# A square-relu MLP whose relu and token factor become one VectorE operation from the accumulators, and two RMS norms at a layer border joined

## The chip, the cores and the metric

The kernel runs on one core of a Trainium2 chip. The metric is the device time of one execution in microseconds, as the median of several runs. PE is TensorE (matmul), PEld its weight load, DVE is VectorE, ACT ScalarE, POOL GpSimd, and SP the engine that issues most of the transfers.

## The reference, cut to what matters

Two model parts run one after the other on 512 tokens of width 1024, in fp32. The first has two layers, each a mixer (attention, then a gated linear attention, GLA) and an MLP; it ends with a norm. The second begins with a norm of its own.

```
def rmsnorm(x, g):
    y = x * rsqrt(mean(x * x, axis=-1) + EPS)
    return y * g

def sq_relu_mlp(h, w_in, w_out):              # 1024 -> 4096 -> 1024
    return square(relu(h @ w_in)) @ w_out

# first part, for each of two layers
h = h + mixer(rmsnorm(h, norm_mix[i]))
h = h + sq_relu_mlp(rmsnorm(h, norm_mlp[i]), mlp_w_in[i], mlp_w_out[i])
# end of the first part, begin of the second
x = rmsnorm(h, final_norm)
hn = rmsnorm(x, norm_g[0]) * (1.0 + sc1) + sh1
y = hybrid_mixer(hn, ...)
x = x + g1 * rmsnorm(y, norm_g[1])
```

`sc1`, `sh1` and `g1` come from a conditioning vector; a matrix product for it, called ada here, is computed on POOL beside the MLPs.

## The kernel before, in words

The program is written out by hand for each engine, with semaphores between them; nothing reorders it. Activations lie transposed: features on the 128 partitions, 8 tiles of 512 tokens. Every fp32 product is made of three faster fp32r matmuls from high and low parts (`three`, L252 to L254): data and weights are split by ACT, which rounds the high part (`split_hi`, L214, for weights), and by DVE, which subtracts (`split_lo`, L222). A weight block is 128x2048 and has two slots. Its users count `block_done`.

**The MLP** has 16 units of 256 hidden features. PE does, in turn, `in(u)` (48 matmuls of 512 columns into two PSUM banks) and `out(u-1)` (four quarters, each of 12 matmuls into two banks, banks 4-5 and 6-7 in turn). A quarter is added to the residual `x` by DVE (`mlp_dve_add`, L808), and quarters 2 and 3 can start only once the add of the quarter two before has freed its banks. The token factor 1/rms of the norm is not in the input of `in`: it is multiplied in afterwards, from `rstd`. For a unit, ACT takes relu from the accumulators into `m_r` (L775), DVE multiplies by `rstd` (L816), DVE squares in place (L818), ACT rounds to `m_hi` (L778), and DVE subtracts to `m_lo` (L825). In its queue DVE has, for each unit: L816, L818, the add of quarter 0, `split_lo` for the next block, the add of quarter 1, L825, the adds of quarters 2 and 3, `split_lo`.

**A norm's sum** is numbered by `n`. ACT squares pairs of tiles (L320); for the numbers in `FOLDED` POOL adds the pairs (L343), and PE then makes 4 matmuls with a matrix of ones (L333) where it would make 8 otherwise. Each is an fp32 matmul, of which the trace shows two instructions. ACT makes `rstd` by Ln and Exp (L348, L349).

**The border** between the parts lies behind the second MLP: sum 4 of the last quarters, `rstd`, then `dve_norm_x` (L387), which writes the normed `x` tile by tile; PE sums up ada (L1200); ACT squares the new `x`, PE makes sum 5 (not folded), ACT makes `rstd` again; then per tile DVE makes a row (L370), ACT rounds it into `h_hi` (L361) and DVE subtracts into `h_lo` (L380), and PE starts on the mixer's first block. The mixer (`mix_*`) has first four blocks with rotary products (`rotate`, L1275), scores of an index head (`index_score`, L1298), whose relu ACT takes (L1480) and DVE adds up, a top-k on DVE, and then 48 attention steps, in which DVE takes the maximum of a step's scores (L1699), ACT its exponential (L1505), and PE fills the time with projection blocks.

Of the kernel before, what the change touches and what calls it, by code (L numbers as in the profile page):

```python
# [23 lines left out]
P = 128  # L24
# [55 lines left out]
def build(nc, xT_d, wb_d, ada_d, prm_d, con_d, rope_d, gup_d, rel_d, sel_d, out_d):  # L80
    with ExitStack() as ctx:
# [70 lines left out]
        with ExitStack() as scope:  # L152
# [14 lines left out]
            with ExitStack() as s2:  # L167
                with ExitStack() as s3:
                    mx.update({n: sb(n, s, F32, s3) for n, s in [("x_qi", [P, 2, S]), ("x_ki", [P, 1, S])]})
                mx.update({n: sb(n, s, d, s2) for n, s, d in [  # L170
                    ("b_q2", [P, 4, S], F32R), ("b_k2", [P, 4, S], F32R), ("b_kl", [P, 4, S], F32R), ("b_v", [P, TT, 4, P], F32),
                    ("c_v", [P, TT, 2, P], F32), ("x_o", [P, 2, S], F32)]})
# [123 lines left out]
        def squares(n):  # L296


            return ff["f_c"] if n == 7 else sq

        FOLDED = (1, 2, 3, 4, 6, 8)
# [81 lines left out]
        def dve_norm_x(dve, n, gain):  # L383

            dve_rstd(dve, n)
            for k in range(KT):
                dve.scalar_tensor_tensor(out=x[:, k, :], in0=x[:, k, :], scalar=gain[:, k:k + 1], in1=rstd[:],  # L387
                                         op0=ALU.mult, op1=ALU.mult).then_inc(n_app, 1)
# [102 lines left out]
        def attn_pe(pe):  # L491
# [224 lines left out]
        m_relu, m_scaled, m_sq, m_hi, m_lo, m_out, m_add = map(sem, ("m_relu", "m_scaled", "m_sq", "m_hi_s", "m_lo_s", "m_out", "m_add"))  # L716
# [52 lines left out]
        def mlp_act_in(act, i, u, par, b, slot, more=True):  # L769
# [107 lines left out]
        def gla_pe(pe, b0, rows):  # L877
# [10 lines left out]
            def within(h):  # L888

                for d in range(2):  # L890
# [338 lines left out]
        X_UNITS = 48  # L1229
        F_LOG, CUM = mx["x_o"][0:4, 0, :], mx["x_o"][0:4, 1, :]  # L1230
# [38 lines left out]
        def mix_pe(pe, b0):  # L1269
# [31 lines left out]
            pe_block(pe, b0, b0 % 2, HH, 0, rows=40)  # L1301
# [7 lines left out]
            rotate(1)  # L1309
            pe.wait_ge(x_raw, 2)  # L1310
# [3 lines left out]
            pe.wait_ge(x_tok, 1)  # L1314
            for k in range(2, KT):
# [116 lines left out]
        def mix_act(act, b0):  # L1432
# [40 lines left out]
            next_hi(act, b0 + 4, b0 % 2)  # L1473

# [99 lines left out]
        def mix_dve(dve, b0):  # L1574
# [132 lines left out]
            for s in range(X_UNITS + 3):  # L1707
# [352 lines left out]
def program(nc, block, e):  # L2060
# [68 lines left out]
    def _(act):  # L2129
# [17 lines left out]
        e["act_std"](act, 3, 6)  # L2147
        e["mlp_act"](act, 1, B_MLP1, 4)
# [15 lines left out]
    def _(dve):  # L2164
# [12 lines left out]
        e["ada_dve"](dve, 0)  # L2177
        e["gla_dve"](dve, B_GLA)
# [16 lines left out]
    def _(pe):  # L2195
# [10 lines left out]
        e["pe_sums"](pe, 5, 2)  # L2206
# [145 lines left out]
```

## Time and profile before

| | us |
|---|---|
| median of 3 runs | 2146.72 (2146.18 to 2148.09) |
| the profiled execution's own time | 2146.94 |
| its span in the trace | 2145.2 |
| PE busy | 2064.4 (96%) |
| DVE busy | 1161.0 (54%) |
| ACT busy | 748.6 (35%) |
| POOL busy | 583.8 (27%) |

The 1.7 us between the span and the time of the same execution lie around the program. A busy share is an average over stages. Idle time of PE is what can be won; work taken from another engine counts only where PE waits for it.

### The profile page before, as it was taken

The numbers are of one execution on the slowest core, as the hardware profiler recorded it, in microseconds if no ns is written. First come the engines' busy times: TensorE is split into PE (matmuls) and PEld (weight loads), VectorE is DVE, ScalarE is ACT, GpSimd is POOL, SyncE is SP. The second block draws the span as 40 slices with busy tenths as digits, with TensorE's granted clock in tenths as the row PEclk, the third lists the DMA queues.
The fourth block names the chain that finished last, engine by engine and source line by source line (L and its number), as shares of the span: only waits on it lengthen the run. The fifth ranks groups of instructions, "written<-read, shape, count | busy, mean of one in ns | idle before, by whom it ended". The sixth has DMA issues, their size and how long they took to land.

```text
span 2145.2 us, 23937 instructions
## 1 busy us (share of the span) xinstructions
PE 2064.4 (96%) x9444; PEld 1641.4 (77%) x9444; DVE 1161.0 (54%) x1163; ACT 748.6 (35%) x783; POOL 583.8 (27%) x478
## 2 busy tenths in 40 slices
PE   8999999999999998999999998999999979999996
PEld 5666777777777887777777776788888858888884
DVE  4687455655655445455655654594235354545455
ACT  4455432222225432332222223345553233322322
POOL 0000189994000000189994001233320000000000
PEclk9999999999999999999999998999999989999998
DMA  4200144442222231134442222132222312222221
GB/s 173 87 20 1 40 150 145 148 148 95 98 79 81 79 98 40 40 141 153 149 146 96 98 79 84 60 79 64 75 79 98 107 51 99 80 96 98 98 98 39
DMA packets 30812, 197.81 MB, mean 92 GB/s; under 512 B 3312, under 2 KB 3440, under 8 KB 7952
## 3 DMA queue, kind: packets, MB, share of 16 engines
q1 hardware_dynamic: 25552, 168.44, 23.0%
q0 software_dynamic: 5184, 28.31, 4.0%
q8 instruction: 53, 0.87, 0.2%
q14 instruction: 23, 0.19, 0.0%
HBM read 191.50 MB, written 2.10 MB: 90 GB/s over the span
## 4 chain that ended last, share of the span: by engine, by line
PE 85%; DVE 7%; issue 4%; ACT 3%; POOL 1%; DMA 0%; DVEq 0%; POOLq 0%; ACTq 0%; SPq 0%
PE ps L252 23%; PE ps L254 22%; PE ps L253 22%; PE ps L551 3%; PE ps L333 2%; DVE x L808 2%; PE ps L538 1%; PE ps L1391 1%; PE ps L283 1%; PE ps L285 1%; PE ps L284 1%; PE ps L941 1%; PE ps L530 1%; PE ps L529 1%; DVE m_r L816 1%
## 5 line engine op out<-in xcount | busy, mean ns | idle before, releaser
L222 DVE TENSOR_TENSOR w_lo<-w_raw,w_hi 128x2048 fp32r<-128x2048 f32 x140 | 326.4, 2332 | 218.1 <-ACT w_hi L214 216.5
L214 ACT ACTIVATE w_hi<-w_raw 128x2048 fp32r<-128x2048 f32 x144 | 275.3, 1912 | 411.7 <-PE ps L254 411.6
L252 PE MATMUL ps<-h_hi,w_hi 128*128 128x512 f32 x944 | 382.2, 405 | 11.8 <-DVE h_lo L380 7.8
L253 PE MATMUL ps<-h_lo,w_hi 128*128 128x512 f32 x944 | 373.6, 396 | 0.0
L254 PE MATMUL ps<-h_hi,w_lo 128*128 128x512 f32 x944 | 372.9, 395 | 0.0
L343 POOL TENSOR_TENSOR sq<-sq 128x1024 f32<-128x1024 f32 x12 | 38.6, 3218 | 857.6 <-ACT sq L320 857.6
L1184 POOL TENSOR_SCALAR ada_t<-ada_w,prm 128x256 f32<-128x256 f32 x192 | 259.1, 1349 | 10.4 <-DMA ada_w<-in_ada 9.5
L252 PEld LDWEIGHTS ps<-h_hi,w_hi 128*128 128x128 f32 x944 | 181.2, 192 | 56.7 <-issue 20.2
L252 PE MATMUL ps<-m_hi,w_hi 128*128 128x512 f32 x512 | 205.4, 401 | 6.5 <-DVE x L808 6.4
L254 PEld LDWEIGHTS ps<-h_hi,w_lo 128*128 128x128 f32 x944 | 180.7, 191 | 39.2
L253 PEld LDWEIGHTS ps<-h_lo,w_hi 128*128 128x128 f32 x944 | 181.3, 192 | 37.5 <-issue 1.4
L252 PE MATMUL ps<-m_xhi,w_hi 128*128 128x512 f32 x512 | 203.6, 398 | 0.0
L254 PE MATMUL ps<-m_xhi,w_lo 128*128 128x512 f32 x512 | 203.3, 397 | 0.0
L254 PE MATMUL ps<-m_hi,w_lo 128*128 128x512 f32 x512 | 203.0, 397 | 0.0
L253 PE MATMUL ps<-m_lo,w_hi 128*128 128x512 f32 x512 | 201.6, 394 | 0.0
L253 PE MATMUL ps<-m_xlo,w_hi 128*128 128x512 f32 x512 | 201.5, 393 | 0.0
L816 DVE TENSOR_TENSOR m_r<-m_r,rstd 128x1024 f32<-128x1024 f32 x32 | 43.2, 1349 | 248.7 <-ACT m_r L775 248.7
L808 DVE TENSOR_TENSOR x<-x,ps 128x1024 f32<-128x1024 f32 x128 | 155.3, 1214 | 30.1 <-PE ps L254 30.1
L1191 POOL TENSOR_TENSOR ada_acc<-ada_acc,ada_t 128x256 f32<-128x256 f32 x168 | 160.5, 956 | 14.0
L775 ACT ACTIVATE m_r<-ps 128x1024 f32<-128x1024 f32 x32 | 32.9, 1027 | 273.4 <-PE ps L254 273.3
L252 PEld LDWEIGHTS ps<-m_hi,w_hi 128*128 128x128 f32 x512 | 96.1, 188 | 41.3 <-DVE x L808 19.9
L253 PEld LDWEIGHTS ps<-m_xlo,w_hi 128*128 128x128 f32 x512 | 96.1, 188 | 25.1 <-issue 1.0
(278 smaller groups left out, 3335.9 us busy)
## 6 DMA issues: line engine op xcount, KB each, us to landing
w_raw<-in_wb SPq DMA_DIRECT2D x154, 1024.0 KB, 4.9
ada_w<-in_ada POOLq DMA_DIRECT2D x24, 1024.0 KB, 5.4
x<-in_xT SPq DMA_DIRECT2D x4, 512.0 KB, 5.1
out_T<-x SPq DMA_DIRECT2D x4, 512.0 KB, 2.8
b_k<-b_k POOLq DMA_DIRECT2D x4, 256.0 KB, 5.5
b_kl<-b_kl POOLq DMA_DIRECT2D x4, 256.0 KB, 6.7
con<-in_con SPq DMA_DIRECT2D x1, 640.0 KB, 11.4
a_kh<-a_kh POOLq DMA_DIRECT2D x2, 256.0 KB, 3.7
```

Of the source, the lines that this page charges most:

```text
L214: act.activation(w_hi[:, slot], w_raw[:, slot], ACT.Copy).then_inc(hi_done, 1)
L222: dve.tensor_tensor(w_lo[:, slot], w_raw[:, slot], w_hi[:, slot].bitcast(F32), ALU.subtract).then_inc(split_done, 1)
L252: pe.matmul(out, w[0], h[0], start=start, stop=False)
L253: pe.matmul(out, w[0], h[1], start=False, stop=False)
L254: return pe.matmul(out, w[1], h[0], start=False, stop=stop)
L333: last = pe.matmul(ps[:, bank, :], ones[:], squares(n)[:, slot, i * S:(i + 1) * S], start=(j == (2 if folded else 0) and i == 0), stop=(j ...
L343: pool.tensor_tensor(sq[:, 0], sq[:, 0], sq[:, 1], ALU.add).then_inc(n_fold, 1)
L551: pe.matmul(ps[:, h % 2, :], at_["a_v"][:, c, kv, :], p_turned[:, half, :][:, c, :], start=c == 0, stop=c == TT - 1).then_inc(a_PV, 1)
L808: dve.tensor_tensor(xd, xd, pair_(2 + q % 2), ALU.add).then_inc(m_add, 1)
L816: dve.tensor_tensor(two(r), two(r), rstd[:].unsqueeze(1).to_broadcast([P, 2, S]), ALU.mult).then_inc(m_scaled, 1)
L1184: pool.tensor_scalar(ml["ada_t"][:, k % 2], w, cact[:, k:k + 1], None, ALU.mult).then_inc(ada_row, 1)
L1191: ins = pool.tensor_tensor(acc, acc, ml["ada_t"][:, k % 2], ALU.add)
```

## The change

It has three parts. **In the MLP**, one `scalar_tensor_tensor` on DVE reads the accumulators and makes max(0, v) times `rstd`; the squares move to ACT, twice: one rounded into `m_hi`, one in place in `m_r`. ACT's relu and copy go, and ACT's weight split stands ahead of both. **At the border**, sum 4 is taken over x squared times the squared gain of `final_norm` plus a small number, so that its `rstd` serves both norms at once; the rows of `h` are made straight from the old `x` with the product of both gains (`G_BOTH`). Sum 5, of plain squares, now folded, gives the factor `x_r4` of the first norm, which only `x` itself needs: its squares stand behind the rows on ACT, its matmuls behind the second rotary product on PE, and `dve_norm_x` is spread over attention steps 32 to 39. **Small things**: the gains and constants lie in columns of the identity matrix `con`, so that transposes use `identr`, a copy; two short helpers make the gains, on DVE ahead of GLA and on ACT ahead of the second MLP.

```diff
+        FOLDED = (1, 2, 3, 4, 5, 6, 8)
...
+            if n == 4:
+                for i in range(2):
+                    ins = act.activation(to[:, i, :], src[:, 2 * j + i, :], ACT.Square, scale=G_ROOT[:, 2 * j + i:2 * j + i + 1])
+            else:
+                ins = act.activation(to, src[:, 2 * j:2 * j + 2, :], ACT.Square)
+            ins.then_inc(n_sq, 1)
...
         def act_std(act, n, bank):
 
             act.wait_ge(n_ssq, ssq_before(n + 1))
-            alink(act, act.activation(rstd[:], ps[:, bank, :], ACT.Ln, bias=pc("eps"), scale=1.0 / D))
-            act.activation(rstd[:], rstd[:], ACT.Exp, scale=-0.5).then_inc(n_std, 1)
+            to = X_R4[:] if n == 5 else rstd[:]
+            alink(act, act.activation(to, ps[:, bank, :], ACT.Ln, bias=EPS2 if n == 4 else pc("eps"), scale=1.0 / D))
+            act.activation(to, to, ACT.Exp, scale=-0.5).then_inc(n_std, 1)
...
+        def dve_norm_x(dve, n, gain, k):
+
+            if k == 0:
+                dve_rstd(dve, n)
+            dve.scalar_tensor_tensor(out=x[:, k, :], in0=x[:, k, :], scalar=gain[:, k:k + 1], in1=X_R4[:],
+                                     op0=ALU.mult, op1=ALU.mult).then_inc(n_app, 1)
+
+        def both_gains_dve(dve):
+
+            gf = pc("final", 0, KT)
+            dve.memset(EPS2, EPS * EPS)
+            dve.tensor_tensor(G_ROOT, gf, gf, ALU.mult)
+            dve.tensor_tensor(G_BOTH, gf, gain2[:, 0, :], ALU.mult).then_inc(g_both, 1)
+            dve.wait_ge(g_both, 1)
+
+        def both_gains_act(act):
+
+            act.wait_ge(g_both, 1)
+            alink(act, act.activation(G_ROOT, G_ROOT, ACT.Ln, bias=pc("eps")))
+            alink(act, act.activation(G_ROOT, G_ROOT, ACT.Exp, scale=0.5))
...
             act.wait_ge(block_done, b + 1)
-            if not (isinstance(u, int) and i == 0 and u < 2):
-                act.wait_ge(m_lo, c - 1)
-            act.activation(ml["m_r"][:, par].rearrange("p (a s) -> p a s", a=2), pair_(par), ACT.Relu).then_inc(m_relu, 1)
             split_hi(act, b + 2, slot)
-            act.wait_ge(m_sq, c + 1)
-            act.activation(ml["m_hi"][:, par], ml["m_r"][:, par].rearrange("p (a s) -> p a s", a=2), ACT.Copy).then_inc(m_hi, 1)
+            act.wait_ge(m_relu, c + 1)
+            r = two(ml["m_r"][:, par])
+            act.activation(ml["m_hi"][:, par], r, ACT.Square)
+            act.activation(r, r, ACT.Square).then_inc(m_hi, 1)
...
-            dve.wait_ge(m_relu, c + 1)
+            dve.wait_ge(block_done, b + 1)
...
-            dve.tensor_tensor(two(r), two(r), rstd[:].unsqueeze(1).to_broadcast([P, 2, S]), ALU.mult).then_inc(m_scaled, 1)
-            dve.wait_ge(m_scaled, c + 1)
-            dve.tensor_tensor(r, r, r, ALU.mult).then_inc(m_sq, 1)
+            if not (isinstance(u, int) and i == 0 and u < 2):
+                dve.wait_ge(m_lo, c - 1)
+            dve.scalar_tensor_tensor(out=two(r), in0=pair_(par), scalar=0.0, in1=rstd[:].unsqueeze(1).to_broadcast([P, 2, S]),
+                                     op0=ALU.max, op1=ALU.mult).then_inc(m_relu, 1)
...
+            pe_ssq(pe, 5, 2, 7)
+            pe_ssq(pe, 5, 3, 7)
             pe.wait_ge(x_raw, 2)
             pe_block(pe, b0 + 3, (b0 + 3) % 2, HH, 1, tiles=range(2))
             pe.wait_ge(x_rot, 2)
             pe.wait_ge(f_raw, 1)
             pe.wait_ge(x_tok, 1)
+            pe.wait_ge(n_std, 6)
...
             next_hi(act, b0 + 4, b0 % 2)
+            act_std(act, 5, 7)
...
                     top_k(8 + s, 9 + s)
+                if 32 <= s < 32 + KT:
+                    dve_norm_x(dve, 5, pc("final", 0, KT), s - 32)
...
+            pool_fold(pool, 5)
             low(b0 + 4)
...
         e["mlp_act"](act, 1, B_MLP1, 4)
         act.preload_act_table_set("natural_log_exp_and_others")
-        e["act_std"](act, 4, 2)
+        e["act_norm_h"](act, 4, 2, 2, shift(0))
         e["renorm_squares"](act, 5, x)
-        e["act_norm_h"](act, 5, 2, 2, shift(0))
...
-        e["dve_norm_x"](dve, 4, gain("final", 0))
+        e["dve_norm_h"](dve, 4, 2, e["G_BOTH"], shift(0))
         e["ada_dve"](dve, 1)
-        e["dve_norm_h"](dve, 5, 2, e["gain2"][:, 0], shift(0))
...
         e["ada_pe"](pe, 1)
-        e["pe_sums"](pe, 5, 2)
         e["mix_pe"](pe, B_MIX)
```

Place one, DVE in the last unit of the second MLP, before (`L808` is the add of a quarter, `L222` a weight's low part; lines are those of the kernel before):

```order
L816 TENSOR_TENSOR m_r<-m_r,rstd 128x1024 [waits m_relu]
L818 TENSOR_TENSOR m_r<-m_r 128x1024 [waits m_scaled]
L808 TENSOR_TENSOR x<-x,ps 128x1024 [waits m_add,m_out]
L222 TENSOR_TENSOR w_lo<-w_raw,w_hi 128x2048 [waits hi_done]
L808 TENSOR_TENSOR x<-x,ps 128x1024 [waits m_add,m_out]
L825 TENSOR_TENSOR m_lo<-m_r,m_hi 128x1024 [waits m_hi_s]
```

And DVE at the same place after the change (lines of the changed kernel: `L836` is the add, `L224` the weight's low part):

```order
L846 SCALAR_TENSOR_TENSOR m_r<-ps,rstd 128x1024 [waits m_lo_s,block_done]
L836 TENSOR_TENSOR x<-x,ps 128x1024 [waits m_add,m_out]
L224 TENSOR_TENSOR w_lo<-w_raw,w_hi 128x2048 [waits hi_done]
L836 TENSOR_TENSOR x<-x,ps 128x1024 [waits m_add,m_out]
L854 TENSOR_TENSOR m_lo<-m_r,m_hi 128x1024 [waits m_hi_s]
```

One instruction stands ahead of the first add where two stood, and it waits for PE (`block_done`), not for ACT.

Place two, DVE at the border before, from the weight split that ends the MLP to the first two low parts of the mixer's input:

```order
L222 TENSOR_TENSOR w_lo<-w_raw,w_hi 128x2048 [waits hi_done]
L387 SCALAR_TENSOR_TENSOR x<-x,prm,rstd 128x512 [waits n_std]
L387 SCALAR_TENSOR_TENSOR x<-x,prm,rstd 128x512 x7
L1207 TENSOR_TENSOR modT<-ps,prm 128x24 [waits ada_sum]
L1209 SCALAR_TENSOR_TENSOR gain<-modT,prm 128x8 [waits dve_chain]
L1209 SCALAR_TENSOR_TENSOR gain<-modT,prm 128x8
L370 SCALAR_TENSOR_TENSOR sq<-x,gain,rstd 128x512 [waits n_std,mod_set]
L370 SCALAR_TENSOR_TENSOR sq<-x,gain,rstd 128x512
L380 SCALAR_TENSOR_TENSOR h_lo<-sq,modT,h_hi 128x512 [waits n_row,n_hi]
```

And DVE there after the change:

```order
L224 TENSOR_TENSOR w_lo<-w_raw,w_hi 128x2048 [waits hi_done]
L382 SCALAR_TENSOR_TENSOR sq<-x,con,rstd 128x512 [waits n_std]
L382 SCALAR_TENSOR_TENSOR sq<-x,con,rstd 128x512
L392 SCALAR_TENSOR_TENSOR h_lo<-sq,modT,h_hi 128x512 [waits n_row,n_hi]
L382 SCALAR_TENSOR_TENSOR sq<-x,con,rstd 128x512
```

The eight operations on `x` and ada's three stand ahead of the rows before; after, the rows come first.

Place three, PE in the mixer behind the second rotary product (`x_g`), after the change; before, the four matmuls on `x_sq` are not there:

```order
L1305 MATMUL ps<-x_g,con 128x512 [waits x_rot_s,x_raw]
L1305 MATMUL ps<-x_g,con 128x512
L344 MATMUL ps<-x_sq,ones 128x512 [waits n_folded]
L344 MATMUL ps<-x_sq,ones 128x512
L344 MATMUL ps<-x_sq,ones 128x512 [waits n_sq]
L344 MATMUL ps<-x_sq,ones 128x512
L254 MATMUL ps<-h_hi,w_hi 128x512 [waits split_done,x_raw]
```

At the border PE loses its eight matmuls of sum 5, which stood between ada and the first block, and gets these four back here.

## Rows read from the trace of the kernel before

**Rows 1.** The page, chain of work that ended last, by engine.

```profile
PE 85%; DVE 7%; issue 4%; ACT 3%; POOL 1%; DMA 0%; DVEq 0%; POOLq 0%; ACTq 0%; SPq 0%
```

**Rows 2.** Waits of PE, whole span: total us, times, longest.

```profile
PE ps L252 <- DVE x L808: 6.4, 15, 0.7
```

**Rows 3.** Timeline of one MLP unit: start, us, what, [idle before <-releaser].

```profile
325.33 1.03 ACT L775 ACTIVATE m_r<-ps 128x1024 f32<-128x1024 f32 x1 [9.22 <-PE ps L254]
...
326.39 1.38 DVE L816 TENSOR_TENSOR m_r<-m_r,rstd 128x1024 f32<-128x1024 f32 x1 [7.92 <-ACT m_r L775]
...
327.80 1.65 DVE L818 TENSOR_TENSOR m_r<-m_r 128x1024 f32<-128x1024 f32 x1
...
329.37 1.21 DVE L808 TENSOR_TENSOR x<-x,ps 128x1024 f32<-128x1024 f32 x1
...
330.50 2.72 DVE L222 TENSOR_TENSOR w_lo<-w_raw,w_hi 128x2048 fp32r<-128x2048 f32 x1
...
333.14 1.21 DVE L808 TENSOR_TENSOR x<-x,ps 128x1024 f32<-128x1024 f32 x1
333.30 0.40 PE L254 MATMUL ps<-m_hi,w_lo 128*128 128x512 f32 x1
...
334.40 0.50 PE L252 MATMUL ps<-m_hi,w_hi 128*128 128x512 f32 x1 [0.70 <-DVE x L808]
```

**Rows 4.** Single lines: duration in ns, min/median/max, of all their instructions.

```profile
L808 DVE TENSOR_TENSOR x<-x,ps x128: 1205/1214/1222, 306.0 to 1288.8; 128x1024 f32<-128x1024 f32 x128
...
L816 DVE TENSOR_TENSOR m_r<-m_r,rstd x32: 1224/1227/1784, 292.3 to 1267.3; 128x1024 f32<-128x1024 f32 x32
...
L1675 DVE SCALAR_TENSOR_TENSOR b_q<-ps,b_q x4: 1218/1222/1227, 1407.0 to 1519.3; 64x1024 fp32r<-64x1024 f32 x4
...
L1629 DVE SCALAR_TENSOR_TENSOR x_o<-x_o x1: 5065/5065/5065, 1364.2 to 1364.2; 4x512 f32<-4x512 f32 x1
...
L412 ACT ACTIVATE m_xhi<-x,prm x16: 704/707/724, 244.9 to 922.6; 128x512 fp32r<-128x512 f32 x16
```

**Rows 5.** Chain of work at the border, in order of time: start, us, what.

```profile
1291.46 5.23 PE ps L333 x8
1296.69 5.63 PE ps L1200 x48
1302.32 9.98 PE ps L333 x16
1312.33 0.70 ACT rstd L348
...
1313.79 0.76 DVE sq L370
...
1315.33 0.76 DVE h_lo L380
...
1316.23 0.77 PE ps L252
```

**Rows 6.** Two windows, engines' busy us; third from last: granted clock.

```profile
1302.20:1308.30 6.10, 6.10 (x9) 2.52 (x10) 1.63 (x5) 1.06 (x1) 2.70 (x2) 0.51 0.55 178
...
1316.20:1321.90 5.70, 5.67 (x13) 4.51 (x14) 5.70 (x9) 2.89 (x4) 0.00 (x0) 0.50 0.00 0
```

**Rows 7.** Timeline of the mixer's first blocks, ACT and PE.

```profile
1330.07 1.03 ACT L1441 ACTIVATE x_g<-ps 128x1024 f32<-128x1024 f32 x1 [5.94 <-PE ps L254]
...
1364.38 0.70 PE L1298 MATMUL ps<-x_ki,x_qi 64*128 64x256 f32 x4 [1.08 <-DVE x_qi L1597]
...
1373.35 0.91 PE L1298 MATMUL ps<-x_ki,x_qi 64*128 64x384 f32 x2 [1.19 <-ACT sq L1480]
```

**Rows 8.** Timeline of attention step 35, DVE and POOL.

```profile
1539.84 4.58 POOL L1726 TENSOR_TENSOR w_lo<-w_raw,w_hi 128x2048 fp32r<-128x2048 f32 x1 [12.58 <-ACT w_hi L1554]
...
1540.01 0.69 DVE L1699 TENSOR_REDUCE con<-ps 128x1 f32<-128x512 f32 x1 [1.35 <-PE ps L1367]
```

**Rows 9.** Transfers issued at the border: KB each, us to landing.

```profile
w_raw<-in_wb SPq DMA_DIRECT2D x3, 1024.0 KB, 7.1
```

More of the change, by code:

```diff
@@ L169, in build @@
                     mx.update({n: sb(n, s, F32, s3) for n, s in [("x_qi", [P, 2, S]), ("x_ki", [P, 1, S])]})
-                mx.update({n: sb(n, s, d, s2) for n, s, d in [
-                    ("b_q2", [P, 4, S], F32R), ("b_k2", [P, 4, S], F32R), ("b_kl", [P, 4, S], F32R), ("b_v", [P, TT, 4, P], F32),
-                    ("c_v", [P, TT, 2, P], F32), ("x_o", [P, 2, S], F32)]})
+                mx.update({n: sb(n, s, d, s2) for n, s, d in [("b_q2", [P, 4, S], F32R), ("b_k2", [P, 4, S], F32R)]})
+                with ExitStack() as s3:
+                    mx["x_sq"] = sb("x_sq", [P, 2, 1024], F32, s3)
+                mx.update({n: sb(n, s, d, s2) for n, s, d in [("b_kl", [P, 4, S], F32R), ("b_v", [P, TT, 4, P], F32),
+                    ("c_v", [P, TT, 2, P], F32), ("x_o", [P, 2, S], F32), ("x_r4", [P, S], F32)]})
             with ExitStack() as s2:
@@ L296, in squares @@
         def squares(n):
-            return ff["f_c"] if n == 7 else sq
-        FOLDED = (1, 2, 3, 4, 6, 8)
+            return {5: mx["x_sq"], 7: ff["f_c"]}.get(n, sq)
+        G_ROOT, G_BOTH = con[:, IDENT + 80:IDENT + 88], con[:, IDENT + 88:IDENT + 96]
+        EPS2 = con[:, IDENT + 96:IDENT + 97]
+        FOLDED = (1, 2, 3, 4, 5, 6, 8)
         def ssq_before(n):
@@ L319, in act_square @@
                 act.wait_ge(n_app, 8 * n)
-            act.activation(squares(n)[:, square_slot(n, j)].rearrange("p (a s) -> p a s", a=2), src[:, 2 * j:2 * j + 2, :], ACT.Square).then_inc(n_sq, 1)
+            to = squares(n)[:, square_slot(n, j)].rearrange("p (a s) -> p a s", a=2)
+            if n == 4:
[4 more added lines that the diff above has]
+            ins.then_inc(n_sq, 1)
         def pe_ssq(pe, n, j, bank):
@@ L342, in pool_fold @@
                     pool.wait_ge(n_fold, 2 * FOLDED.index(n) + 1)
-                pool.tensor_tensor(sq[:, 0], sq[:, 0], sq[:, 1], ALU.add).then_inc(n_fold, 1)
+                pool.tensor_tensor(squares(n)[:, 0], squares(n)[:, 0], squares(n)[:, 1], ALU.add).then_inc(n_fold, 1)
         def act_std(act, n, bank):
             act.wait_ge(n_ssq, ssq_before(n + 1))
-            alink(act, act.activation(rstd[:], ps[:, bank, :], ACT.Ln, bias=pc("eps"), scale=1.0 / D))
-            act.activation(rstd[:], rstd[:], ACT.Exp, scale=-0.5).then_inc(n_std, 1)
+            to = X_R4[:] if n == 5 else rstd[:]
+            alink(act, act.activation(to, ps[:, bank, :], ACT.Ln, bias=EPS2 if n == 4 else pc("eps"), scale=1.0 / D))
+            act.activation(to, to, ACT.Exp, scale=-0.5).then_inc(n_std, 1)
         def dve_rstd(dve, n):
@@ L381, in dve_norm_h @@
                                                  op0=ALU.add, op1=ALU.subtract).then_inc(n_app, 1)
[L383 to L388, printed above, removed]
+        def dve_norm_x(dve, n, gain, k):
[13 more added lines that the diff above has]
+            alink(act, act.activation(G_ROOT, G_ROOT, ACT.Exp, scale=0.5))
+        g_both = sem("g_both")
         def dve_norm_add(dve, n, gain):
@@ L532, in turn @@
             def turn(u):
+                if u == 0:
+                    pe.wait_ge(ident_set, 1)
                 pe.wait_ge(a_exp, u + 1)
@@ L537, in turn @@
                     w = slice(c * P, (c + 1) * P)
-                    last = pe.transpose(ps[:, 2 + u % 2, w], trow[:, u % 4, w], mat(IDENT))
+                    last = pe.transpose(ps[:, 2 + u % 2, w], trow[:, u % 4, w], identr[:].bitcast(F32))
                 last.then_inc(a_T, 1)
@@ L901, in within @@
                         w = slice(t * P, (t + 1) * P)
-                        last = pe.transpose(ps[:, bank + 1, w], gl["g_kd"][:, d, w], mat(IDENT))
+                        last = pe.transpose(ps[:, bank + 1, w], gl["g_kd"][:, d, w], identr[:].bitcast(F32))
                     last.then_inc(g_kT, 1)
@@ L1229, in build @@
         X_UNITS = 48
+        X_R4, X_SQ = mx["x_r4"], mx["x_sq"]
         F_LOG, CUM = mx["x_o"][0:4, 0, :], mx["x_o"][0:4, 1, :]
@@ L1299, in index_score @@
                           start=True, stop=True).then_inc(i_S, 1)
-            pe_block(pe, b0, b0 % 2, HH, 0, rows=40)
+            pe_block(pe, b0, b0 % 2, HH, 0, rows=32)
+            pe.wait_ge(mod_set, 2)
             pe_block(pe, b0 + 1, (b0 + 1) % 2, HH, 1)
```

4 lines of the change are left out of this document (3 added, 1 removed).

## The prediction, on record before the changed kernel ran

> **What bounds the kernel now.** I read the page first: PE is busy for 96% of the span, and the chain that ended last lies on PE for 85% of it, on DVE for 7% [rows 1]. Only two kinds of gain are open: idle time of PE, and PE work that goes. So I took the waits of PE, and looked where this change touches one. In the MLPs PE waits for the adds of L808, 15 times, 6.4 us [rows 2]. At the border the chain shows what stands between the last MLP matmul and the mixer's first block: sum 4, ada, sum 5, `rstd`, the first row, its low part [rows 5]. `dve_norm_x` isn't on it: sum 5's matmuls are, and those of its first half run at a granted clock of 0.51 [rows 6].
>
> **The MLP's wait.** Rows 3 show one unit with the longest wait. PE ended `in(u)` at about 325.1. ACT's relu follows at 325.33; then DVE's L816 (1.38) and L818 (1.65), so that the add of quarter 0 begins at 329.37, though its quarter (12 matmuls at 0.233 us) was done by 328.1. Behind it the weight's low part takes 2.72 and the add of quarter 1 starts at 333.14 and ends at 334.35. Quarter 3 needs its banks; its first matmul starts at 334.40, where 333.30 + 0.23 = 333.53 was possible. It costs 0.87, and the step to the second matmul is 0.34 instead of 0.23, so 0.97 in all: 0.27 more than the 0.70 that the row calls idle.
>
> After the change, one operation starts at 325.33. The trace has no such form in fp32 of 128x1024 from the accumulators; nearest is L1675, the same operation with one input from PSUM, 1.22 [rows 4]. I take 1.22, ending at 326.6. The first add is then bound by its quarter: 328.15 instead of 329.37, 1.2 us earlier. Low part and second add move with it, the add to 333.1, which is 0.4 ahead of 333.53. Even if the new operation took double, 2.45, it would end at 327.8 and cost nothing. So the 15 waits go: 6.4 + 15 x 0.27 = 10.4. I add 1 for restarts that are late by less than 0.1 and have no named wait; the last unit of each MLP keeps its small wait, since there quarter 0's add is behind a weight split that PE itself releases. I take **-11**; bounds: -6.4 (only the named idle) and -13.
>
> ACT loses a relu of 1.03 and a copy of 1.06 and gets two squares of that size; its weight split starts 1 us earlier. `m_hi` and the squares are ready some 4.2 us after `in(u)`, while DVE comes to L825 only behind the second add, 9 us after it: hidden. That L825 now waits for both squares costs nothing for the same reason. The accumulators are freed by DVE instead of ACT; behind them is `in(u+2)`, two blocks later, and DVE was idle for 7.92 before L816 [rows 3].
>
> **The border.** (a) Away go PE's 9.98 of sum 5, and `rstd`, the first row and its low part from behind it, since they now follow sum 4 while ada runs: ada's end at 1302.32 to the first block at 1316.23 is 13.91 [rows 5]. After sum 4 come Ln and Exp (1.4), and row, high and low part (2.3 from 1313.79 to 1316.09), 3.8 together, against ada's 5.63: PE comes free last and the block starts right behind ada. Later tiles come every 1.3 us; at half clock PE takes 6 x 0.43 = 2.6 for a tile. No wait. (b) Squares of sum 4 are made in halves with a factor per partition. Nearest row: L412, 0.707 each [rows 4], so 1.41 for a pair against 1.06. Two pairs lie in series with the folds: **+0.7**. (c) PE ran at half clock for 6.1 us behind ada and 5.7 behind the idle stretch [rows 6], this is the lower of its two levels, 1.2 GHz. The block now stands behind ada, so I take the 6.1: +0.2. Together -13.91 + 0.7 + 0.2 = **-13.0**.
>
> (d) Sum 5 comes back as four fp32 matmuls, eight instructions at 0.43 us (the second half of sum 4's eight in rows 5 ran so): +3.4 on PE in the mixer. PE there waits 1.08 for DVE's x_qi and later 1.19 for an index relu [rows 7]; its lateness takes both up. Left: **+1.1**. PE also waits for `n_std` there. ACT's Ln and Exp for it come behind its weight split, about 1.6 us before PE, delayed as above, gets there: nothing. If the chain behind (top-k on DVE, whose start hangs on PE's block) had slack, it would be 0; if none of the two waits were taken up, 3.4.
>
> (e) On ACT, sum 5's squares come between `h_hi` and x_g (L1441): 4 x 1.06, and two folds on POOL of 2.4 in series, 9 us from about 1309, so x_g starts at 1318.3. The first block ends near 1316.7, so x_g is 1.6 late against 1330.07 [rows 7]. PE wants it only behind the second block, 10.9 later. Then the weight split for the third block: its transfer is behind `n_app` 40, now reached with the last low part at 1309.7, not at 1303.5. With four smaller transfers to issue ahead of it, about 2 us, and 7.1 to land [rows 9] it is there at 1319, split by 1324; PE wants it at 1329. Hidden, with 5 us in hand.
>
> (f) `dve_norm_x`, 8 x 0.745, one in each of steps 32 to 39. DVE's smallest idle time before L1699 in these steps is 1.35 [rows 8]: it fits, 0. The gains' helpers (some 0.2 us each) lie where DVE and ACT are idle. Transposes with `identr` are of the same kind as before: 0.
>
> At (f) a row speaks against a plain reading of durations. L1629 took 5.07 us for 4x512 elements [rows 4], starting while POOL subtracted a weight's low part. L808, with one input in PSUM, never took over 1.222, L816, with both in SBUF, up to 1.784. The Trainium skill, page "SBUF — State Buffer", section "Who interferes with whom", says that a VectorE instruction with two SBUF inputs and a GpSimd one that reads SBUF exclude each other for a whole instruction. `dve_norm_x` has two SBUF inputs, and step 35's would be issued at 1540.7, in POOL's 1539.84 to 1544.42 [rows 8]. Held until then, it ends at 1545.2; the next maximum is 1.2 late and ACT's exponential ends 0.3 before PE needs it at 1546.3. By the rule the sum would be 0 to 1 us worse here; by the idle row alone, the same as above. For the MLP the rule and the rows agree that the new operation, with one SBUF input, isn't lengthened.
>
> **Sum.** -11 - 13.0 + 1.1 = -22.9. The profiled execution took 2146.9 (span 2145.2 and 1.7 around it), 0.2 over the median: 2124.0, against the median 2123.8. I say **2124**.
>
> **Rivals.** *A: the MLPs keep their waits*, all or half, because the weight's low part between the adds is held up by POOL's ada work (2.72 in rows 3): MLP term 0 to -6, time 2129 to 2135. For it: ada runs beside the units with the long waits. Against: add 0 gains a fixed 1.2, more than the longest loss of 0.97. Chance 0.15. *B: the border's gain shrinks in the mixer*: index scores, top-k and weight splits are a chain of DVE, ACT and POOL, and sum 5 is on ACT and PE in front of it. If the 5 us in hand of (e) are overdrawn by as much, or (d) costs its whole 3.4 and ACT's Ln and Exp 1.4 too, 4 to 9 us are lost: 2128 to 2133. Chance 0.17. *C: slower*: DVE's new operation is itself held by POOL in nearly each unit, because its reading of `rstd` does contend. With a duration X, add 1 ends at 325.33 + X + 1.2 + 2.4 + 1.2 = 330.1 + X, against 333.5: a wait of X - 3.4. To eat both gains, 11 and 12 us, over 30 units it must be 0.77 each, so X from 4.2 up decides. At L1629's 5.07 [rows 4] it is 1.67, 50 us in all: 2147 - 23 + 50 = 2174. Against it: L816, with both inputs in SBUF, is at 1.78 at worst [rows 4]. Chance 0.03. *D: nothing in sight* (A and B at their worst together, within 0.2%, that is 4.3 us, about what a measurement of this kernel can tell from no change): 0.03. My forecast, 2119 to 2128: 0.62.
>
> **Range.** Lowest: -13 in the MLP, -13.4 at the border, (d) at 0: 2120, and 2 for unknown small ones, 2118. Upwards it takes in most of A and B: 2134. Faster 0.94, same 0.03, slower 0.03.
>
> **What the trace after will show.** PE's waits for the add gone or below 1 us in sum; the new operation at 1.22; the first add starting with its quarter. First mixer block 0.1 to 0.3 behind ada's last matmul, sum 4 0.7 later than before, Ln starting before ada ends. Four matmuls on `x_sq` taking 3.4 behind the second rotary product, and no wait of PE for `rstd` behind them. The maxima of steps 33 to 40 at their old distances. I am wrong if the new operation is above 3 us, if PE waits for `h_lo` in the first block, or for a weight block behind it.

## The result, and the profile after

| | before | after |
|---|---|---|
| median, us | 2147.4 (2146.2 to 2151.4) | 2117.9 (2115.0 to 2123.1) |
| ratio | | 0.9865 (95%: 0.9846 to 0.9885) |
| the profiled execution's span | 2145.2 | 2121.2 |
| PE busy | 2064.4 (96%) | 2051.5 (97%) |
| DVE busy | 1161.0 | 1120.1 |

The change gained 29.5 us where I had forecast 23. The page's chain, to be read against [rows 1], lies on PE for 91%, and DVE's share has fallen by 3:

```profile
PE 91%; DVE 4%; ACT 2%; issue 1%; POOL 1%; DMA 0%; POOLq 0%; ACTq 0%; DVEq 0%; SPq 0%
```

The profiled execution of the changed kernel took 2123.1, the longest of its four. The table cuts both traces where ACT starts the Ln of a norm, where DVE starts the last add of the second MLP, and where PE starts the first block of the mixer:

| stretch, us | before | after | difference | forecast |
|---|---|---|---|---|
| start to first Ln | 15.87 | 16.35 | +0.5 | |
| attention | 273.98 | 270.61 | -3.4 | 0 |
| first MLP | 362.35 | 356.87 | -5.5 | with the next MLP row, -11 |
| GLA and projection | 281.76 | 282.41 | +0.6 | 0 |
| second MLP, Ln to last add | 354.87 | 348.79 | -6.1 | |
| border, last add to first mixer block | 27.40 | 17.25 | -10.2 | -13.0 |
| first mixer block to the Ln of sum 6 | 420.55 | 420.63 | +0.1 | +1.1 |
| the rest of the span | 408.42 | 408.29 | -0.1 | 0 |

**The MLP after**, timeline of one unit, in the columns of [rows 3]:

```profile
321.96 1.23 DVE L846 SCALAR_TENSOR_TENSOR m_r<-ps,rstd 128x1024 f32<-128x1024 f32 x1 [6.90 <-PE ps L256]
...
324.76 1.22 DVE L836 TENSOR_TENSOR x<-x,ps 128x1024 f32<-128x1024 f32 x1 [1.57 <-PE ps L256]
...
325.90 2.55 DVE L224 TENSOR_TENSOR w_lo<-w_raw,w_hi 128x2048 fp32r<-128x2048 f32 x1
...
328.37 1.21 DVE L836 TENSOR_TENSOR x<-x,ps 128x1024 f32<-128x1024 f32 x1
```

DVE has finished the new operation at 323.2 and then idles 1.57 until PE is done with quarter 0: the first add starts with its quarter. The second add starts 6.4 behind `in(u)`, where it was 7.8 in [rows 3]. The longest waits of PE no longer have the add among them:

```profile
PE ps L344 <- POOL sq L354: 8.7, 3, 3.2
PE ps L344 <- ACT sq L330: 8.1, 2, 7.4
PE ps L970 <- DVE g_s L1138: 8.0, 4, 2.7
```

and the new operation is as long as I took it (durations in ns, min/median/max), whatever POOL does beside it:

```profile
L846 DVE SCALAR_TENSOR_TENSOR m_r<-ps,rstd x32: 1223/1225/1226, 288.4 to 1252.4; 128x1024 f32<-128x1024 f32 x32
```

**The border after**, from the chain, to be read against [rows 5]: POOL's second fold, sum 4, ada, first block.

```profile
1275.81 2.35 POOL sq L354
1278.20 6.66 PE ps L344 x8
1284.87 7.42 PE ps L1229 x48
1292.28 0.64 PE ps L254
```

Sum 5, `rstd`, row and low part are gone from between ada and the block. Ln, Exp, row, high and low part run beside ada and are done 3.7 us before the block:

```profile
1284.90 0.69 ACT L360 ACTIVATE rstd<-ps,con 128x512 f32<-128x512 f32 x1 [2.23 <-PE ps L344]
...
1287.83 0.75 DVE L392 SCALAR_TENSOR_TENSOR h_lo<-sq,modT,h_hi 128x512 fp32r<-128x512 f32 x1
```

But sum 4 took 6.66 instead of 5.23 and ada 7.42 instead of 5.63, with the same instructions. The windows (last columns: granted clock, DMA share, GB/s) show why:

```profile
1277.50:1284.50 7.00, 6.29 (x8) 2.69 (x9) 2.29 (x1) 4.42 (x4) 0.65 (x1) 0.52 0.01 2
1284.50:1287.50 3.00, 3.00 (x27) 2.79 (x26) 1.21 (x2) 1.74 (x3) 0.00 (x0) 1.00 0.00 0
1287.50:1297.60 10.10, 10.10 (x37) 8.94 (x37) 9.81 (x17) 6.27 (x10) 2.69 (x2) 0.51 0.00 0
```

Nearly all of sum 4, the last 4.7 us of ada and the first 5.6 of the block ran at the lower level, 1.2 GHz, which I call half clock below. The trace before has such stretches here too: the two of [rows 6], and one more at the start of sum 4, which the prediction's clock term leaves out:

```profile
1291.10:1294.60 3.50, 3.14 (x4) 1.51 (x5) 0.21 (x1) 3.08 (x3) 0.30 (x1) 0.51 0.02 5
```

**`dve_norm_x` in attention step 35**, DVE and POOL, where [rows 8] stood:

```profile
1515.96 4.58 POOL L1763 TENSOR_TENSOR w_lo<-w_raw,w_hi 128x2048 fp32r<-128x2048 f32 x1 [12.59 <-ACT w_hi L1589]
1516.14 0.69 DVE L1734 TENSOR_REDUCE con<-ps 128x1 f32<-128x512 f32 x1 [0.57 <-PE ps L1401]
1516.74 4.36 DVE L399 SCALAR_TENSOR_TENSOR x<-x,prm,x_r 128x512 f32<-128x512 f32 x1
...
1521.02 0.28 DVE L1734 TENSOR_REDUCE con<-ps 128x1 f32<-128x128 f32 x1
```

The operation that takes 0.74 where POOL is idle was under way for 4.36 and ended 0.56 us after POOL's subtraction. The next one of the eight, in step 36, took 1.58, and it too ended behind a POOL operation with two inputs:

```profile
1520.51 1.75 POOL L1775 TENSOR_TENSOR x_ylo<-x_o,x_yhi 128x512 fp32r<-128x512 f32 x1
1521.22 1.58 DVE L399 SCALAR_TENSOR_TENSOR x<-x,prm,x_r 128x512 f32<-128x512 f32 x1
```

### The profile page after: what moved, and what is told of

Same layout as the page of the kernel before. It is cut to its first block, busy times and chain, and to the rows that moved or that the text cites. A ratio compares the mean times of both kernels' runs of the same rounds, so it can differ in the third digit from the quotient of the medians.

```text
span 2121.2 us, 23916 instructions
## 1 busy us (share of the span) xinstructions
PE 2051.5 (97%) x9436; PEld 1642.1 (77%) x9436; DVE 1120.1 (53%) x1134; ACT 747.2 (35%) x789; POOL 548.6 (26%) x480
## 4 chain that ended last, share of the span: by engine, by line
PE 91%; DVE 4%; ACT 2%; issue 1%; POOL 1%; DMA 0%; POOLq 0%; ACTq 0%; DVEq 0%; SPq 0%
PE ps L254 25%; PE ps L256 25%; PE ps L255 25%; PE ps L580 3%; PE ps L344 2%; PE ps L567 1%; PE ps L1425 1%; PE ps L285 1%; PE ps L287 1%; PE ps L286 1%; PE ps L1229 1%; PE ps L970 1%; PE ps L556 1%; PE ps L557 1%; ACT w_hi L216 1%
## 5 line engine op out<-in xcount | busy, mean ns | idle before, releaser
L224 DVE TENSOR_TENSOR w_lo<-w_raw,w_hi 128x2048 fp32r<-128x2048 f32 x140 | 324.8, 2320 | 218.1 <-ACT w_hi L216 216.5
L1213 POOL TENSOR_SCALAR ada_t<-ada_w,prm 128x256 f32<-128x256 f32 x192 | 222.0, 1156 | 9.8 <-DMA ada_w<-in_ada 8.9
L836 DVE TENSOR_TENSOR x<-x,ps 128x1024 f32<-128x1024 f32 x128 | 155.7, 1216 | 93.3 <-PE ps L256 93.3
L846 DVE SCALAR_TENSOR_TENSOR m_r<-ps,rstd 128x1024 f32<-128x1024 f32 x32 | 39.2, 1225 | 218.1 <-PE ps L256 218.1
L254 PEld LDWEIGHTS ps<-m_xhi,w_hi 128*128 128x128 f32 x512 | 96.1, 188 | 24.2 <-issue 1.0
## 6 DMA issues: line engine op xcount, KB each, us to landing
con<-in_con SPq DMA_DIRECT2D x1, 640.0 KB, 12.3
```

What stands on the lines that cost most here:

```text
L224: dve.tensor_tensor(w_lo[:, slot], w_raw[:, slot], w_hi[:, slot].bitcast(F32), ALU.subtract).then_inc(split_done, 1)
L254: pe.matmul(out, w[0], h[0], start=start, stop=False)
L836: dve.tensor_tensor(xd, xd, pair_(2 + q % 2), ALU.add).then_inc(m_add, 1)
L846: dve.scalar_tensor_tensor(out=two(r), in0=pair_(par), scalar=0.0, in1=rstd[:].unsqueeze(1).to_broadcast([P, 2, S]), op0=ALU.max, op1=ALU. ...
L1213: pool.tensor_scalar(ml["ada_t"][:, k % 2], w, cact[:, k:k + 1], None, ALU.mult).then_inc(ada_row, 1)
```

## The experiments

The theory to be tested: the gain is made of the MLPs' waits and of the work between sum 4 and the first block, as forecast, and what lies over or under it is the granted clock, which differs between executions of one kernel. Rivals: the copied identity made the attention shorter; the halved squares or the order make sum 4 and ada dearer for good; sum 5 costs nothing wherever it stands.

For this I also summed, over windows of 4 or 5 us (1 us at the border), their length times (1 - granted clock): the **clock loss** of an execution, what it would have been shorter by at full clock if PE had worked all through. Idle time of PE at the lower level is counted too, and windows round, so it is good to about 1 us. Where not said otherwise, the edits are to the changed kernel.

**1. The changed kernel once more.** No edit.

> The changed kernel once more, to see how far its executions spread and why. Theory (clock): the border costs more in an execution in which PE's slow spell covers all of sum 4 and ada (6.7 and 7.4 us) than in one in which it covers only part of them, so the median over this kernel lies 0 to 7 us under its profiled 2123, at about 2118, and the spread of its runs is some 8 us. Rival (fixed cost): sum 4 and ada take 14 us in each execution because of the halved squares and the order of the work; then a second profile shows 6.6 and 7.4 again, and the spread has another place.

Measured: 2120.2 (2116.6 to 2124.5), ratio to before 0.9884 (0.9866 to 0.9903), and before itself from 2142.3 to 2151.5 in 15 runs. The profiled span is 2114.6, 6.6 shorter than the first one. The chain at the same place, then the window of the only half-clock stretch at the border:

```profile
1276.88 2.35 POOL sq L354
1279.28 3.70 PE ps L344 x8
1282.98 5.46 PE ps L1229 x48
1288.43 0.64 PE ps L254
```

```profile
1287.50:1291.30 3.80, 3.80 (x14) 3.22 (x14) 3.80 (x6) 1.96 (x3) 2.70 (x2) 0.55 0.00 0
```

Border 12.3 instead of 17.25, with nothing edited. The rival of a fixed cost falls. Clock loss of the whole span: 39.7 in the first profile, 32.6 here; what is left is 2081.5 and 2082.0.

**2 to 4. The parts alone**, each put into the kernel before.

```diff
# 2: the MLP hunks of the change alone; 3: all the others
# 4: only these two
-                    last = pe.transpose(ps[:, 2 + u % 2, w], trow[:, u % 4, w], mat(IDENT))
+                    last = pe.transpose(ps[:, 2 + u % 2, w], trow[:, u % 4, w], identr[:].bitcast(F32))
...
-                        last = pe.transpose(ps[:, bank + 1, w], gl["g_kd"][:, d, w], mat(IDENT))
+                        last = pe.transpose(ps[:, bank + 1, w], gl["g_kd"][:, d, w], identr[:].bitcast(F32))
```

> The kernel before with the MLP part alone. Theory: PE's 15 waits for the add and the small late restarts go, -11 to -12 us, about 2135. Rival (the parts help each other): the weight splits and the border set how much of it is seen, and alone it brings less than 8.

> The kernel before with the border's part, sum 5's new place, the helpers and the identity's copy, but not the MLP part. Theory: -13 by my prediction's sum if sum 4 and ada keep their 5.2 and 5.6 us; -10 if they run at half clock throughout as in the profile after. With nothing lost in the mixer that is 2134 to 2137. Rival (something outside the border gave the 3.4 us in the attention): -13 to -17, and the attention is again some 3 us shorter.

> The kernel before, only with the transposes of attention and GLA taking the copied identity. Theory (nothing): a transpose takes its 270 ns as before, 0 us. Rival (this is what made the attention 3.4 us shorter in the profile after): -3 us, and the stretch from the first norm's Ln to that of the MLP is 3 us shorter in this profile too. If the 3.4 us are the clock's, the stretch varies from one execution to the next with no edit.

| | median, us | ratio to before | span | clock loss | rest |
|---|---|---|---|---|---|
| before (first profile) | | 1 | 2145.2 | 42.8 | 2102.4 |
| 4, identity | 2149.0 | 1.0006 (0.9994 to 1.0019) | 2149.5 | 46.4 | 2103.1 |
| 2, MLP | 2131.7 | 0.9925 (0.9910 to 0.9940) | 2133.4 | 41.4 | 2092.0 |
| 3, border | 2130.5 | 0.9926 (0.9912 to 0.9939) | 2136.3 | 43.2 | 2093.1 |
| both (first profile) | 2117.9 | 0.9865 (0.9846 to 0.9885) | 2121.2 | 39.7 | 2081.5 |

The identity's copy does nothing that can be seen. The attention took 271.54 with it alone (4) and 271.54 without it (2); over the 14 profiles it is 270.3 to 274.0, and the 273.98 of the first one before is the longest. My -3.4 there is no effect of the change. Of the MLP part, the first MLP shows the size best: 356.86 in (2) against 363.60 and 363.38 in (3) and (4), and the second one, Ln to last add, 348.80 against 354.83 and 355.24. In (3) the border took 17.1, with sum 4 at 6.62 and the same half-clock stretches as in the first profile after, though the MLP was the old one: the long border does not come from the MLP part. A short one without that part was not profiled.

By the medians, before at 2146.3, (2) brings 14.6 and (3) 15.8, each more than I expected; by the last column they bring 10.4 and 9.3. Most of the remainder is clock loss: over its five executions each of the two has some 37 us of it, and the kernel before some 41. The two gains add up: 0.9925 x 0.9926 = 0.9852, inside the interval of the whole change.

**5. Ada ahead of sum 4** (second MLP).

```diff
             mlp_out(pe, i, u, u % 2, b0 + 2 * u + 1, (b0 + 1) % 2, after=after)
+            if i == 1:
+                ada_pe(pe, 1)
             pe_ssq(pe, n, 2, 2)
...
-        e["ada_pe"](pe, 1)
```

> The changed kernel with ada's 48 short matmuls behind the second MLP put ahead of the last two sums' matmuls, into the 3.2 us in which PE waits for POOL's folds. Theory: sum 4 starts when it did or up to 2 us later, and behind it only Ln, Exp, row, high and low part (3.8 us) stand before the first block, instead of ada's 5.6 to 7.4; if the clock holds, sum 4 itself takes 3.4 to 5.2 instead of 6.7. So 2 to 7 us less than the changed kernel, about 2113. Rival: what is before the first block is set by the clock alone; ada at 5.6 in front delays sum 4 by 2.4, and less than 2 us is won.

Measured: 2121.4 (2118.9 to 2123.6), 0.9888 (0.9869 to 0.9908): the same as (1), not the 2113 that I expected. The rival held, by arithmetic and not by the clock: at full clock ada takes 5.25, 2.0 more than the idle 3.2 that it fills, and behind the sum 3.86 of idle time come back in place of ada's 5.2, together +0.6. The trace has 14.3 from last add to first block, 1.7 of it clock loss: 12.6 against 12.0 in (1).

**6. PE kept busy ahead of sum 4.**

```diff
+            if i == 1:
+                for _ in range(14):
+                    pe.matmul(ps[:, 3, 0:P], ones[:], ones[:], start=True, stop=True)
             pe_ssq(pe, n, 2, 2)
```

> The changed kernel with 14 idle fp32 matmuls of 128 columns, whose result is thrown away, put where PE waits for POOL's folds ahead of the last two sums' matmuls; the work behind is the same. Theory (clock): they keep PE at its upper level, so sum 4 takes about 3.5 to 5 and ada 3 to 5.6 instead of 6.7 and 7.4, and the first block starts 2 to 7 us earlier. Rival (fixed cost of the order or of the halved squares): the two keep 14 us together, and the kernel is the same or up to 1 us slower.

Measured: 2118.6 (2116.6 to 2120.7), 0.9874 (0.9853 to 0.9894). The 28 instructions fill 1277.21 to 1280.50 of 3.3 us; sum 4 takes 3.70, ada 5.55, as in (1), which had no filling. So the profile fits the theory, but does not tell it from chance: without the filling sum 4 is at full clock in some executions too.

**7 and 8. More work on DVE in each MLP unit.** One further new operation ahead of the real one, then three.

```diff
+            for j, to in enumerate((trow[:, 0:2], trow[:, 2:4], trow[:, 0:2])):      # (7) has the first alone
+                if j == 2:
+                    dve.wait_ge(m_extra, c + 1)
+                ins = dve.scalar_tensor_tensor(out=to, in0=pair_(par), scalar=0.0, in1=rstd[:].unsqueeze(1).to_broadcast([P, 2, S]),
+                                               op0=ALU.max, op1=ALU.mult)
+                if j == 0:
+                    ins.then_inc(m_extra, 1)
             dve.scalar_tensor_tensor(out=two(r), in0=pair_(par), scalar=0.0, in1=rstd[:].unsqueeze(1).to_broadcast([P, 2, S]),
                                      op0=ALU.max, op1=ALU.mult).then_inc(m_relu, 1)
```

> The changed kernel with one more of DVE's new MLP operation (1.22 us, into a free buffer) ahead of the real one in each unit. By the prediction's rule, a wait for the second add of X - 3.4 us with X what DVE does from the end of in(u) to the first add, X is 2.45 and nothing is lost: 0 to 1 us. Rival (DVE has no such slack, the 6.4 us of waits before were its edge): 0.3 to 1 us in each of 30 units, 10 to 30 us in all.

> As the last, with three more, X = 4.9 us. By the rule X - 3.4 = 1.5 us of wait per unit, and 0.3 more for each restart at the slower step, in 30 units: 45 to 54 us slower than the changed kernel, 2163 to 2172. Rival (the slack is larger than the rule has it, since the weight split or the low part behind gives way): under 20 us. Rival (the weight split is late too and a second wait comes on top): over 70.

Measured: (7) 2120.5 (2119.7 to 2123.1), 0.9885 (0.9866 to 0.9904), first MLP 356.85: nothing, as the rule says. (8) 2156.5 (2150.9 to 2159.4), 1.0042 (1.0030 to 1.0054), slower than before. One unit of (8), DVE and PE, and PE's wait for the add over the whole span:

```profile
372.30 3.48 DVE L850 SCALAR_TENSOR_TENSOR sq<-ps,rstd 128x1024 f32<-128x1024 f32 x3 [6.96 <-PE ps L256]
375.71 1.21 DVE L854 SCALAR_TENSOR_TENSOR m_r<-ps,rstd 128x1024 f32<-128x1024 f32 x1
376.84 1.21 DVE L837 TENSOR_TENSOR x<-x,ps 128x1024 f32<-128x1024 f32 x1
...
378.10 0.50 PE L254 MATMUL ps<-m_hi,w_hi 128*128 128x512 f32 x1 [0.33 <-DVE x L837]
...
381.63 0.50 PE L254 MATMUL ps<-m_hi,w_hi 128*128 128x512 f32 x1 [0.46 <-DVE x L837]
```

```profile
PE ps L254 <- DVE x L837: 18.3, 60, 0.5
```

Each MLP is 17.2 longer (374.08 against 356.87 for the first), 34.4 in all and 1.15 in each of 30 units, less than the 45 to 54 us I expected. Two slips of mine explain it. Four operations of 1.21 start 1.13 apart, so the first add starts X = 376.84 - 372.30 = 4.54 behind `in(u)`, not 4.9; and X - 3.4 = 1.14 is the whole delay of quarter 3, to which nothing is to be added. The other way of counting agrees: 60 named waits of 18.3 and 60 restarts of 0.27 are 34.5. So the rule of the rival C gives 1.14 from this one unit where the mean of 30 is 1.15, and the 0.27 of my MLP term comes out again.

**9. Ada split** at both borders. **10. Half a fold**: POOL adds only the first two pairs of sums 2 and 4.

```diff
# 9
+            ada_pe(pe, i, 0, 13)
             pe_ssq(pe, n, 2, 2)
...
+        e["ada_pe"](pe, 1, 13, 24)
# 10
+        HALF = (2, 4)
...
-            for j in (1, 2):
+            for j in (1,) if n in HALF else (1, 2):
...
+            if n in HALF:
+                for slot, first in ((0, True), (1, False)) if j == 2 else ((0, False),):
...
+                    for i in range(2):
+                        last = pe.matmul(ps[:, bank, :], ones[:], squares(n)[:, slot, i * S:(i + 1) * S],
+                                         start=(first and i == 0), stop=(j == 3 and i == 1))
```

> The changed kernel with 13 of ada's 24 columns ahead of the last two sums' matmuls and 11 behind them, at both MLPs. At full clock ada takes 5.2 and sum 4 3.4. Ahead of the sum 2.8 us fit into PE's idle 3.2; behind it 2.4 are left, beside Ln, Exp, row, high and low part, 3.8. So PE has 3.8 between sum and first block instead of 5.2, twice: -1.4 us each, -2.8 in all. Rival (the clock decides): the new idle 1.4 us brings further slow stretches, and no gain is seen or a loss of up to 4. Both are near what the times can tell; the stretches of the profile, with their slow time taken off, must show the 1.4.

> The changed kernel in which POOL adds only the first two pairs of squares of sums 2 and 4; the third and the fourth pair go to PE as they are, so that it makes 6 matmuls instead of 4 and waits for no second fold. From the end of the MLP's last matmul: now 3.2 idle and 3.4 for the sum, 6.6; then 1.7 for each of three pairs without idle time, 5.1: -1.5 us at each of two borders. Rival (clock): with PE's idle time gone the slow stretches at the border are gone too, and 2 to 4 us more are won. Rival: the fourth pair's squares are late, since they wait for the first matmul pair to free their slot, and nothing is won.

Measured: (9) 2118.2 (2117.8 to 2119.7), 0.9869 (0.9850 to 0.9887). PE's idle time ahead of the first block is 1.51 as worked out, but the sum ran at half clock (6.54), and half-clock stretches cover 1275.5 to 1283 and 1285.5 to 1293: the border took 13.6, more than the shortest of the changed kernel's, 12.2, and less than its 17.1. Without the clock loss it is 9.6 against 11.3 to 12.0 for the changed kernel, so the expected 1.4 is there, but this execution gave it back in clock, and the median does not show the 2.8 of both borders. (10) 2115.9 (2112.6 to 2117.7), 0.9855 (0.9838 to 0.9873), span 2111.9, the shortest of all. Its chain at the border:

```profile
1272.67 5.19 PE ps L351 x12
1277.86 6.46 PE ps L1249 x48
```

The sum follows the MLP's last matmul with no idle time and ran wholly at full clock; ada did not:

```profile
1272.70:1281.50 8.80, 8.80 (x47) 5.81 (x47) 4.69 (x4) 6.85 (x9) 0.00 (x0) 1.00 0.01 2
1281.50:1288.50 7.00, 7.00 (x25) 6.13 (x25) 6.87 (x12) 3.88 (x6) 2.70 (x2) 0.51 0.00 0
```

The border is 11.5, 0.7 shorter than the best before it in spite of more clock loss (1.3 against 0.2); without the clock loss it is 10.2 against 11.3 to 12.0 for the changed kernel. The rival that the fourth pair is late falls, since PE does not wait for it. The intervals of (10) and of the changed kernel overlap, so it is not shown to be faster, only to have 1.1 to 1.8 less between MLP and mixer, by a measure that is good to about 1 us.

**11 and 12. The price of sum 5's matmuls in the mixer**: two of them left out, then 16 in place of four. The first norm's factor is then another one.

```diff
# 11
-            for i in range(2):
+            for i in range(1 if n == 5 else 2):
# 12
+            for rep in range(7 if n == 5 and j == 3 else 1):
+                for i in range(2):
```

> The changed kernel with two of sum 5's four matmuls, 1.7 us less on PE in the mixer (half of the squares are left out of the first norm's factor). Theory of my prediction: the two waits of PE behind them take up 2.3 of the 3.4 us, so with 1.7 less these waits come back by as much, and the gain is 0 to 0.6. Rival (each us of sum 5 counts in full): -1.7.

> The changed kernel with sum 5's matmuls 16 instead of 4, 12 x 0.86 = 10.3 us more on PE (the second half of the squares is counted seven times in the first norm's factor). Theory (all slack is used up by the four): +10.3. Rival (the index head's chain on DVE and ACT behind has more slack than two waits show, which is why the four cost nothing): +5 or less.

Measured: (11) 2118.2 (2114.6 to 2118.9), 0.9867 (0.9849 to 0.9886); (12) 2126.7 (2126.3 to 2129.0), 0.9909 (0.9890 to 0.9928). The stretch from the first block to the Ln of sum 6, in three executions with the same half-clock stretch at the border: 417.97 in (1), 417.92 in (11), 428.22 in (12). The first 1.7 us taken away bring nothing, and 10.3 more cost 10.25. (The median of (12) is only 6.5 to 8.8 above those of the changed kernel; its profile without the clock loss is 10 longer, 2091.8.) In the chain of (12) they stand in full:

```profile
1329.36 1.72 PE ps L1306 x4
1331.08 13.73 PE ps L345 x32
```

## Why the prediction was right in sign and 4 to 6 us short

**The MLP term** (-11) was right in its mechanism and too small. All 15 waits are gone; the MLPs gained 11.6 in the first pair of profiles. With the clock loss taken off, the first MLP gained some 6.7 (362.4, 361.9 and 361.7 without the part, 355.1 to 355.6 with it), and the second 6.1: -12.8. The term of the sum that was too small is that of the restarts that are late by less than 0.1: I had put 1 us for them, and 12.8 - 10.4 leaves 2.4. My bound of -13 held.

**The border term** (-13.0) was right in what it removed and what takes its place: Ln to low part hidden beside ada, no wait for `h_lo`, and the halved squares at 1.33 for a pair against 1.06, 0.27 each and so +0.5 in series instead of +0.7. Wrong was the step that sum 4 and ada keep their 5.23 and 5.63, with a clock term of +0.2. At full clock they take some 3.7 and 5.25, at half clock up to 6.66 and 7.42. In the eight profiles whose border is that of the changed kernel, the stretch is 17.1 in three ((3), (8) and the first; 17.25 by the chain), 12.2 to 12.3 in four ((1), (6), (11) and (12)) and 13.9 in (7), mean 14.3. The three with the old border have 27.4, 27.4 and 29.2, mean 28.0. So the border is worth 10 to 17, on average -13.7, and the profile that I compared first happened to have the long form.

That -13.7 lies so near to -13.0 is in part luck. Without the clock loss, from the end of the last add to the first block, the border fell from 20.3 to 20.5 us to 10.1 to 10.8: about 10 us are what the change does to it. The other 3 of my term are a half-clock stretch that I counted as gone with sum 5. In the long form it is not gone: PE is at half clock for 3.4, 6.9 and 6.9 us before, and for 6.9 and 10.3 after, 17.2 both times. In the short form only one stretch of 3.4 is left. The mean over both forms happens to lie near what I took off for one stretch.

**(d)**, sum 5's matmuls, forecast at +1.1, cost 0.1 in the first pair of profiles and 0.2 to 0.5 with the clock loss taken off (416.0 before; 416.2 to 416.5 after). I took up 2.3 of the 3.4 by PE's two waits; in fact about 3 are taken up. (11) shows that at least two of the matmuls are free, (12) that there is nothing left behind the four. Both waits are gone from the trace after. In (11) they are back with only 0.17 and 0.43, so what takes up the rest is not shown.

**(e) and (f)** at 0: right. The last square of sum 5 ended at 1305.78 and x_g started at 1306.01, behind PE and not 1.6 late. The Ln of sum 5 starts at 1339.94, right behind its matmuls, and PE does not wait for it. In step 35 POOL held `dve_norm_x` up and the next maximum came 0.96 late, forecast at 1.2; the one behind that starts at 1523.05, 6.91 after the maximum of step 35, exactly as in the trace before (1546.92 - 1540.01). This was the rule of the Trainium skill, page "SBUF — State Buffer", section "Who interferes with whom", and the 4.36 us in step 35 and the 1.58 in step 36, each ending 0.54 to 0.56 behind POOL's operation, bear it out. What I had worked out as its upper limit, 1 us, was not reached: the price in time was 0. For the MLP the same rule left the new operation alone, which has `rstd` from SBUF and the other input from PSUM, and it never took over 1.226.

**Together**: -12.8 - 13.7 + 0.3 = -26.2, from 2146.9 to 2120.7. This sum takes the border with its half-clock stretches and the mixer without them. As the traces have it, the stretch from the first block to the Ln of sum 6 is 420.3 to 420.6 with the old border, 420.6 to 420.8 behind a long new one and 417.9 to 418.0 behind a shorter one in (1), (6) and (7): on average 1.2 less in place of 0.3 more. So it is -27.7, to 2119.2, between the medians of the changed kernel's two measurements, 2117.9 and 2120.2. Of the 6 us by which the first of them lies under my value (and 0.08 under my low bound), the MLP explains 1.8, the stretch behind the border 2.3 and the border's mean 0.7. The rest is the spread of executions, about 9 us for either kernel, of which each median has only four to fifteen.

Each execution on record has its mean granted clock beside it. The means are 2146.7 for 35 executions of the kernel before and 2119.4 for 8 of the changed one, 27.3 less, and their clock losses are about 41 and 37 us. So at least 4 us of the gain are less time at half clock, and 21 (by the profiles) to 23 are the rest. Why the clock loss fell is not shown; (2) and (3) alone have about 37 too.

**The rivals.** A (waits stay) is refuted by the trace. B's mechanism, a mixer that gives the gain back, is refuted by the stretch behind the first block. C's price was tested by (7) and (8) and holds; its condition, X over 4.2, is not met at 1.22. D fell with A and B.

What stays open: why the same program runs 3.4 us at half clock in this place in one execution and 17 in another. (6) tried the idle time ahead of sum 4 and could not tell. Open too is why the clock loss was lower by 4 us with either part.

## What to carry to other kernels

When one execution's trace is compared with another's, take the clock loss off first: it differed by 7 us between two executions of one kernel, as much as a whole term of a sum, while the rest agreed to 0.5. But look also at how much clock loss either kernel has over many executions: part of a gain can lie there. A delay that hides behind a pipeline has a threshold that can be worked out from one timeline (here X - 3.4); two runs on either side of it confirm the arithmetic for the price of one edit. And before work is moved into idle time, compare its length with the hole and with what it was hiding at its old place: ada did not fit into 3.2 us and had covered 3.8.

## What the runs showed of the hardware

- Stretches of PE at the lower of its two levels (granted clock 0.5), 3.4 to 10.3 us long, stand at this border in all 14 profiles. They lie behind idle time of PE, but also in ada, whose 48 instructions have one column each: in (10) PE had no idle time ahead of it and the clock fell 3.6 us into it, and in (6), with the idle time filled, it fell near ada's end.
- Execution times of one kernel spread over 9 us (2142.3 to 2151.5 in 15 runs of before). The two profiles of the changed kernel differ by 6.6 us, and by 0.5 once the clock loss is taken off.
- A `scalar_tensor_tensor` with two SBUF inputs took 4.36 instead of 0.74 while POOL subtracted a weight's low part, in all 12 profiles that have the operation there (4.355 or 4.356), and the next one took 1.58 beside a shorter POOL operation.
- Four such operations of 1.21 us from PSUM, behind each other without a wait, start 1.13 apart: durations of single rows add up to more than the stretch.
